# Gate and up products of feed-forward steps 2 to 10 written turned (weights stationary), in a two-block float32 transformer kernel

## The reference

```
def swiglu(x, w_gate_up, w_down):
    g, u = jnp.split(x @ w_gate_up, 2, axis=-1)
    return (jax.nn.silu(g) * u) @ w_down

x = layer_norm(ALPHA * x + mixed, ln1_g[i], ln1_b[i])
x = layer_norm(ALPHA * x + swiglu(x, w_gate_up[i], w_down[i]), ln2_g[i], ln2_b[i])
```

## Time and profile before

| | us |
|---|---|
| median of 3 runs | 1559.26 (1557.5 to 1559.66) |
| span of the profiled execution | 1558.9 |
| TensorE busy | 1537.2 |
| VectorE busy | 1084.7 |
| ScalarE busy | 757.7 |

### The profile page before, as it was taken

How to read it: one execution, slowest core, us unless ns; L and a number is a source line. 1 busy time by engine, 2 the same in 40 slices (tenths; PEclk the granted TensorE clock), 3 DMA queues, 4 the chain that set the end, 5 groups by cost and what they waited for, 6 DMA issues and landing times.

```text
span 1558.9 us, 19900 instructions
## 1 busy us (share of the span) xinstructions
PE 1537.2 (99%) x8187; PEld 1274.7 (82%) x8187; DVE 1084.7 (70%) x1422; ACT 757.7 (49%) x963; POOL 52.7 (3%) x89
## 2 busy tenths in 40 slices
PE   9999999999999999999999999999999999999997
PEld 7887788888878888888788888877888888978986
DVE  6876967656677776675966756888767677567764
ACT  5646544443444434346644343566444434474463
POOL 1100000000000000000000000000100000000010
PEclk9999999999999999999999999999999999999999
DMA  8752567645425766452476664533766546433530
GB/s 317 246 205 79 204 230 256 268 163 189 163 82 197 274 246 255 147 202 96 176 243 243 243 221 152 202 109 136 266 256 233 225 164 223 162 110 147 217 122 27
DMA packets 45898, 299.87 MB, mean 192 GB/s; under 512 B 5540, under 2 KB 5796, under 8 KB 12528
## 3 DMA queue, kind: packets, MB, share of 16 engines
q1 hardware_dynamic: 39600, 278.74, 48.9%
q0 software_dynamic: 5776, 19.01, 3.7%
q10 hardware_dynamic: 432, 0.85, 0.1%
HBM read 296.20 MB, written 2.65 MB: 192 GB/s over the span
## 4 chain that ended last, share of the span: by engine, by line
PE 85%; DVE 8%; ACT 3%; issue 2%; DMA 1%; SPq 0%; POOL 0%; POOLq 0%; DVEq 0%; ACTq 0%
PE psum L1305 53%; PE psum L1264 15%; PE psum L1299 7%; PE psum L1164 3%; DVE w_low L1779 2%; PE psum L1234 1%; PE psum L1428 1%; PE psum L1321 1%; PE psum L1382 1%; PE psum L1416 1%; PE psum L1302 1%; ACT w_high L1533 1%; DMA kv_outside<-arena 1%; DVE xt_low L1813 0%; DVE x_rows L1877 0%
## 5 line engine op out<-in xcount | busy, mean ns | idle before, releaser
L1533 ACT ACTIVATE w_high<-w_raw 128x2048 fp32r<-128x2048 f32 (+1 forms) x240 | 456.5, 1903 | 236.2 <-DMA w_raw<-in_weights 148.9
L1779 DVE TENSOR_TENSOR w_low<-w_raw,w_high 128x2048 fp32r<-128x2048 f32 (+2 forms) x240 | 530.0, 2214 | 34.1 <-ACT w_high L1533 33.3
L1305 PE MATMUL psum<-w_high,xt_high 128*128 128x512 f32 (+1 forms) x1376 | 379.3, 396 | 1.0 <-DVE x_rows L1877 0.8
L1305 PE MATMUL psum<-w_high,xt_low 128*128 128x512 f32 (+1 forms) x1376 | 368.8, 388 | 0.3 <-DVE xt_low L1813 0.3
L1305 PE MATMUL psum<-w_low,xt_high 128*128 128x512 f32 (+1 forms) x1376 | 368.1, 388 | 0.0
L1305 PEld LDWEIGHTS psum<-w_high,xt_low 128*128 128x128 f32 x1376 | 257.9, 188 | 54.9 <-DVE xt_low L1813 0.7
L1305 PEld LDWEIGHTS psum<-w_low,xt_high 128*128 128x128 f32 x1376 | 257.4, 188 | 53.9 <-DVE w_low L1765 0.4
L1305 PEld LDWEIGHTS psum<-w_high,xt_high 128*128 128x128 f32 x1376 | 250.4, 189 | 51.9 <-DVE x_rows L1877 2.4
L2109 DVE TENSOR_TENSOR arena<-arena,psum 128x256 f32<-128x256 f32 x88 | 37.0, 420 | 203.9 <-ACT arena L1665 203.5
L1665 ACT ACTIVATE arena<-psum 128x256 f32<-128x256 f32 x88 | 33.7, 383 | 217.6 <-PE psum L1305 217.6
L1264 PE MATMUL psum<-w_high,ht_high 128*128 128x512 f32 x352 | 99.9, 401 | 0.0
(11 more groups left out here) (250 smaller groups left out, 1486.2 us busy)
## 6 DMA issues: line engine op xcount, KB each, us to landing
w_raw<-in_weights SPq DMA_DIRECT2D x260, 1024.0 KB, 4.8
norm_params<-in_ln_g POOLq DMA_DIRECT2D x8, 512.0 KB, 4.1
norm_params<-in_ln_b POOLq DMA_DIRECT2D x8, 512.0 KB, 5.7
w_raw<-in_weights SPq DMA_DIRECT2D x4, 656.0 KB, 6.0
kv_outside<-arena POOLq DMA_DIRECT2D x3, 512.0 KB, 5.6
mem_kv<-kv_outside POOLq DMA_DIRECT2D x3, 512.0 KB, 3.6
norm_params<-mods_outside POOLq DMA_DIRECT2D x3, 512.0 KB, 6.7
x_rows<-in_x SPq DMA_DIRECT2D x4, 256.0 KB, 5.3
```

Of the source, the lines that this page charges most:

```text
L1305: m = e.matmul(psum[:, bank, 0:w], rows[:, kk, rb * P:rb * P + P], right[:, at:at + w], start=first, stop=last)
L1533: e.activation(K.w_hi[:, g % RING, 0:w], K.w_raw[:, r, 0:w], ACT.Copy).then_inc(K.high.hit(t), 1)
L1779: m = e.tensor_tensor(K.w_lo[:, s, 0:n], K.w_raw[:, r, 0:n], K.w_hi[:, s, 0:n].bitcast(F32), ALU.subtract)
```

## The change

Steps 2 to 10 of each feed-forward part (9 x 4 = 36 steps) take `block_up` in place of `block`. The high and low turned rows become one tensor, `xt_both`. Product n of a half (n is the half of the 256 hidden columns) makes gate and up of 128 hidden columns, turned, in two banks. First come 8 matmuls with `w_hi` stationary (128 x 128) and 512 columns moving, the 256 high and the 256 low turned rows side by side; then 8 with `w_lo` stationary and the 256 high rows moving, added to the first half of the bank. So columns 0 to 255 of a bank hold high x high + low x high, and columns 256 to 511 high x low. Product 0 uses both banks of ring `gemms`, product 1 both banks of ring `tr`.

`gate_turned` replaces `gate`: ScalarE copies columns 256 to 511 of both banks to `ff_rest`; VectorE adds columns 0 to 255 for gate and then for up, and each addition frees its bank; ScalarE takes silu of the gate sum after the first addition; VectorE multiplies. The result is turned already. From step 2 on `split_h` replaces `turn_h`: no transposes, the same high and low halves read from `ff_h`.

`ada_row` moves from right after the block to behind the down products of the step.

```
+    def block_up(self, layer, step, gen):
+        uses = [(ring.take(), ring.take()) for ring in (self.gemms, self.tr)]
+        for half in range(2):
+            t = self.tile("w_gate_up", layer, step, "up", 4 * half)
+            for n in range(2):
+                self.gemm(t, n, half, gen, ("gemm", "turn")[n], uses[n], "up")
+                if half:
+                    self.add("gate_turned", Up(layer, step, n, uses[n], t))
+                self.on()
...
         def turn(step):
-            self.ff_turn[layer, step] = self.tr.take()
-            self.add("turn_h", (layer, step))
+            if step < BY_ROWS:
+                self.ff_turn[layer, step] = self.tr.take()
+                self.add("turn_h", (layer, step))
+            else:
+                self.add("split_h", (layer, step))
...
-        for step in range(2, FF_STEPS):
+        for step in range(BY_ROWS, FF_STEPS):
             if step == 2:
                 self.add("ada_ones", layer)
-            self.block("w_gate_up", layer, step, gen, gate(step), "up")
-            self.ada_row()
+            self.block_up(layer, step, gen)
...
-            if step == 9 and layer in (1, LAST):
-                self.add("modulation", layer // 2)
             turn(step - 1)
             if step < FF_STEPS - 1:
                 if step > 2:
                     t = down_tile(step - 3)
                     for rb in range(RB):
                         down(step - 3, t, rb)
                         self.on()
+                self.ada_row()
+                if step == 9 and layer in (1, LAST):
+                    self.add("modulation", layer // 2)
                 if 2 < step < 9:
                     self.ada_tile()
...
+    def gemm_up(j, hi, lo):
+        ring = (K.gemms, K.tr)[j.rb]
+        if j.half == 0:
+            for use in j.use:
+                pe.wait_ge(*ring.free(use))
+        banks = [psum[:, ring.place(use), :] for use in j.use]
+        for r in range(RB):
+            use = plan.xt_uses[j.gen, r, j.half]
+            pe.wait_ge(*K.xt_high.at(use))
+            pe.wait_ge(*K.tr.out(use))
+        work = [(4 * j.half + k, b, k * BLK + b * FF_STEP + j.rb * P) for k in range(4) for b in range(2)]
+        pe.wait_ge(*K.high.at(j.tile))
+        for kk, b, c in work:
+            e.matmul(banks[b].rearrange("p (n s) -> p n s", n=2), hi[:, c:c + P], K.xt_both[:, :, kk, :], start=kk == 0, stop=False)
+        pe.wait_ge(*K.taken.at(j.tile))
+        for kk, b, c in work:
+            m = e.matmul(banks[b][:, 0:SEQ], lo[:, c:c + P], K.xt_both[:, 0, kk, :], start=False, stop=kk == KC - 1)
+        m.then_inc(K.multiplied.hit((j.tile, j.rb)), 1)
```

ScalarE's part of `gate_turned`, and then VectorE's:

```
+    def gate_turned(j):
+        ring = (K.gemms, K.tr)[j.n]
+        first = min(ring.place(use) for use in j.uses)
+        act.wait_ge(*K.multiplied.at((j.tile, j.n)))
+        if j.step > BY_ROWS:
+            act.wait_ge(*K.h_made.at((j.layer, j.step - 1, j.n)))
+        e.activation(K.ff_rest[j.n], psum[:, first:first + 2, SEQ:BLK], ACT.Copy).then_inc(K.rest_out.hit((j.layer, j.step, j.n)), 1)
+        act.wait_ge(*ring.out(j.uses[0]))
+        e.activation(K.ff_silu[j.step % 2][:, j.n, :], K.ff_gate(j), ACT.Silu).then_inc(K.silu_done.hit((j.layer, j.step, j.n)), 1)
...
+    def gate_turned(j):
+        ring = (K.gemms, K.tr)[j.n]
+        v.wait_ge(*K.rest_out.at((j.layer, j.step, j.n)))
+        for use, row in zip(j.uses, (K.ff_gate(j), K.ff_up(j))):
+            e.tensor_tensor(row, psum[:, ring.place(use), 0:SEQ], row, ALU.add).then_inc(ring.sem(use), 1)
...
+        v.wait_ge(*K.silu_done.at((j.layer, j.step, j.n)))
+        e.tensor_tensor(K.ff_h[j.step % 2][:, j.n, :], K.ff_silu[j.step % 2][:, j.n, :], K.ff_up(j),
+                        ALU.mult).then_inc(K.h_made.hit((j.layer, j.step, j.n)), 1)
```

More of the change, by code:

```diff
@@ L39 @@
 FF_STEPS = D_FF // FF_STEP
+BY_ROWS = 2
 ALPHA = float((2 * len(KINDS)) ** 0.25)
@@ L53 @@
 N_TILES = (3 * KINDS.count("A") + len(KINDS) * (2 * (5 + 1 + 2) + 3 * FF_STEPS) + DEPTH_2 * 2 * (6 + 8 + 2))
-BOTH = ("turned", "memory", "tail", "queries")
+BOTH = ("turned", "memory", "tail", "queries", "up")
 BESIDE = MEMW + IDX_H + HD
@@ L145 @@
 Ff = namedtuple("Ff", "layer step rb use tile")
+Up = namedtuple("Up", "layer step n uses tile")
 Ada = namedtuple("Ada", "row use")
@@ L1246, in gemm @@
         hi, lo = K.w_hi[:, s, :], K.w_lo[:, s, :]
+        if j.kind == "up":
+            gemm_up(j, hi, lo)
+            return
         if j.kind == "down":
@@ L1257, in gemm @@
                 elif n == 1:
-                    pe.wait_ge(*K.tr.out(plan.ff_turn[j.gen[1], j.half]))
+                    pe.wait_ge(*(K.tr.out(plan.ff_turn[j.gen[1], j.half]) if j.half < BY_ROWS
+                                 else K.ht_low.at((j.gen[1], j.half))))
                 else:
@@ L1675, in turn_h, with split_h @@
                      ACT.Copy).then_inc(K.ht_high.hit(j), 1)
+    def gate_turned(j):
[7 more added lines that the diff above has]
+        e.activation(K.ff_silu[j.step % 2][:, j.n, :], K.ff_gate(j), ACT.Silu).then_inc(K.silu_done.hit((j.layer, j.step, j.n)), 1)
+    def split_h(j):
+        layer, step = j
+        if step > 3:
+            act.wait_ge(*K.multiplied.at((plan.down_tile[layer, step - 4], 1)))
+        for n in range(2):
+            act.wait_ge(*K.h_made.at((layer, step, n)))
+        e.activation(K.ht_hi[step % 4], K.ff_h[step % 2], ACT.Copy).then_inc(K.ht_high.hit(j), 1)
     def ada_halves(row):
@@ L1746, in scalar_program @@
               "turn": turn, "dots": dots, "exps": exps, "recip": recip, "turn_prob": turn_prob, "weigh": weigh, "mix_split": mix_split,
-              "gate": gate, "turn_h": turn_h, "ada_halves": ada_halves, "rms": rms, "ret_weigh": ret_weigh, "sb_scores": sb_scores,
+              "gate": gate, "turn_h": turn_h, "gate_turned": gate_turned, "split_h": split_h, "ada_halves": ada_halves, "rms": rms, "ret_weigh": ret_weigh, "sb_scores": sb_scores,
               "sb_halves": sb_halves, "sb_later": sb_later, "sb_split": sb_split, "final": final,
@@ L2116, in turn_h, with split_h @@
                         K.ht_hi[at].bitcast(F32), ALU.subtract).then_inc(K.tr.sem(use), 1)
+    def gate_turned(j):
[3 more added lines that the diff above has]
+            e.tensor_tensor(row, psum[:, ring.place(use), 0:SEQ], row, ALU.add).then_inc(ring.sem(use), 1)
+        if j.step - 2 < BY_ROWS:
+            v.wait_ge(*K.turned.at(plan.ff_turn[j.layer, j.step - 2]))
+        else:
+            v.wait_ge(*K.ht_low.at((j.layer, j.step - 2)))
+        v.wait_ge(*ring.out(j.uses[1]))
+        v.wait_ge(*K.silu_done.at((j.layer, j.step, j.n)))
+        e.tensor_tensor(K.ff_h[j.step % 2][:, j.n, :], K.ff_silu[j.step % 2][:, j.n, :], K.ff_up(j),
+                        ALU.mult).then_inc(K.h_made.hit((j.layer, j.step, j.n)), 1)
+    def split_h(j):
+        at = j[1] % 4
+        v.wait_ge(*K.ht_high.at(j))
+        e.tensor_tensor(K.ht_lo[at], K.ff_h[j[1] % 2], K.ht_hi[at].bitcast(F32),
+                        ALU.subtract).then_inc(K.ht_low.hit(j), 1)
     def ada_ones(layer):
@@ L2287, in vector_program @@
               "choose": choose, "scores": scores, "recip": recip, "turn_prob": turn_prob, "weigh": weigh, "mix_split": mix_split, "gate": gate,
-              "turn_h": turn_h, "ada_ones": ada_ones, "ada_halves": ada_halves, "ada": ada, "modulation": modulation, "norm_rows": norm_rows, "rms": rms,
+              "turn_h": turn_h, "gate_turned": gate_turned, "split_h": split_h, "ada_ones": ada_ones, "ada_halves": ada_halves, "ada": ada, "modulation": modulation, "norm_rows": norm_rows, "rms": rms,
               "modulate": modulate, "rotate": rotate, "ret_scores": ret_scores, "ret_norm": ret_norm,
@@ L2474, in __init__ @@
         self.w_lo = sb("w_low", [P, RING, TW], F32R)
-        self.xt_hi = sb("xt_high", [P, KC, SEQ], F32R)
-        self.xt_lo = sb("xt_low", [P, KC, SEQ], F32R)
+        self.xt_both = sb("xt_both", [P, 2, KC, SEQ], F32R)
+        self.xt_hi, self.xt_lo = self.xt_both[:, 0, :, :], self.xt_both[:, 1, :, :]
         self.x = sb("x_rows", [P, RB, D])
@@ L2520, in __init__ @@
         self.ada_acc = ff[12:14]
+        self.ff_rest = [work[:, BLK * n:BLK * n + BLK].rearrange("p (b s) -> p b s", b=2) for n in range(2)]
         self.prob = [work[:, 1024 * n:1024 * n + 1024] for n in range(2)]
@@ L2609, in __init__ @@
         self.divided, self.mixed_high, self.mixed_low = signal("divided"), signal("mixed_high"), signal("mixed_low")
-        self.silu_done, self.ht_high = signal("silu_done"), signal("ht_high")
+        self.silu_done, self.ht_high, self.ht_low = signal("silu_done"), signal("ht_high"), signal("ht_low")
+        self.rest_out, self.h_made = signal("rest_out"), signal("h_made")
         self.ld_scale, self.ld_norm_g, self.ld_shift = signal("ld_scale"), signal("ld_norm_g"), signal("ld_shift")
@@ L2715, in group_on_scalar, with ff_gate, ff_up @@
         return 0 if by_rows(j) and self.unit_pieces(j) > 4 else None
+    def ff_gate(self, j):
```

(5 more changed lines are left out.)

## The result

The changed kernel takes 1604.23 us (1604.08 to 1606.92), the kernel before 1559.39 us. The ratio is 1.0297, 95% interval 1.0284 to 1.0310: slower by 45 us, where 26 were forecast.

What follows compares the result with a forecast made beforehand. TensorE, busy 99% of the span, was taken to bound the kernel. Span 1558.9 - 8.3 (TensorE's work) + 20.4 (ada row) + 13.6 (start of a part) = 1584.6, with 0.4 to the median 1585.0 us; range 1568 to 1606.

Steps and rivals of the forecast that it cites:

- rival C: TensorE's granted clock falls behind each of 12 new idle times, 1.7 us each: 1605 us; chance 16%.
- TensorE's own work: Blocks of 36 steps cost 7.6 us more, the transposes removed save 15.8 us: net 8.3 us less.
- The chain behind a product: VectorE's queue after a block runs 1.6 us later in every step, free in steps without an ada row.
- rival D: VectorE's queue has no room left and some 27 steps slip by 0.5 to 1 us: 1600 to 1612; chance 6%.
- The ada row: Next block's second product waits for VectorE's late ada addition in steps 5 and 7 of four parts: 20.4 us.
- The start of a part: At steps 1 to 3, TensorE idles 0.46, 2.43 and 0.5 us for banks: 3.4 us per part, 13.6 in all.
- The wait for `ht_low`: At the start of each part, a product wants the bank of step 1's transposes: 0.5 us idle.
- The clock: TensorE's granted clock after new idle times: a fall costs 1.7 us, but the sum included none.
- Rival A: The bank waits don't bite and only TensorE's matmul and transpose savings count: 1551 us; chance 7%.

Runs made afterwards that it cites:

- e7: The kernel before with the four transposes of steps 2 to 10 made twice into the same bank: 1573.94 us against 1557.88.
- e3: The changed kernel with the ada row between the two down products and the transposes of step 1 ahead of the block of step 2: 1556.68 us.
- e4: The changed kernel with 8 more matmuls (a repeated high-weight pass) just ahead of each wait for the ada row, 64 in all: 1596.29 us.
- e2: The changed kernel with the transposes of step 1 ahead of the block of step 2, not behind it: 1590.36 us.
- e1: The changed kernel with the ada row between the two down products of its step, not behind both: 1569.93 us.
- e5: The changed kernel with the ada row back right behind the block, turned products kept: 1592.02 us.

## Why the prediction was right or wrong

Sign, mechanism and places were right; the central number lay 19 us low, and the range held the result at its upper end (1604 of 1606), for the most part for the reason that rival C gave. That it held it was in part luck: 4 of the 12 long waits brought no fall of the clock, and had they brought one too, at some 1.45 us each, the time would have been some 1610 us, outside the range.

- **TensorE's own work**: forecast -8.3 us. The block measured 11.14 instead of 11.09 (36 x 0.26 = 9.4 us more), the transposes -15.8, confirmed by e7 as -16.1: -6.4 to -6.7. e3 with its small waits left comes out 1.9 us under the kernel before. The 13 ns per matmul that the rows of before showed held: the Trainium skill's 2.5 ns (TensorE: Matmul & The Clock Gate, "Back-to-back issue gap") doesn't agree with this trace. By it the whole would have come out some 6 us lower, and the row was the better guide. The Trainium skill gives that figure for a single isolated matmul, which the prediction left out, and these matmuls stand in a stream.
- **The chain behind a product**: `low` at T + 2.39, measured T + 2.40. A step without an ada row lost nothing, so rival D (no room on VectorE) didn't happen; VectorE still idled 1.76 us between two gates.
- **The ada row**: 8 waits of 2.55 us forecast, 2.75 measured, 22.0 us in all against 20.4. Step 9 lost nothing, as forecast.
- **The start of a part**: 2.43 us forecast, 2.58 measured (10.3 us), and 0.5 us at the gate of step 1. The wait for `ht_low` was put at 0.5 us in four parts and was 0.4 in two: in the other two parts the clock had fallen, and TensorE came to the bank too late to wait for it.
- **The clock**: this is the step that failed. The sum took no fall of the clock, and rival C, with 12 falls and 16%, was judged by "full blocks stand on both sides". 8 of 12 waits brought one. One costs some 1.45 us (3.51 against 2.06 for the same eight matmuls), less than the 1.7 of the forecast, since part of the low clock falls into the idle time (the clock was 0.60 over 275 to 276 us, and TensorE began only at 275.50); e4 saved 7.9 us at the six of the ada rows.

Together: -6.4 for TensorE's own work and 35.1 for the four groups of waits make 28.7 us, and the span grew by 43.4. The 14.7 us between are for the most part the clock's: 8 falls x 1.45 us are 11.6, one of them lasted twice as long (some 1.4 more), and 1.7 us are left. They are of the size of what the list of waits doesn't count: from the start of the eight 256-column matmuls at 271.64 to the next start at 275.50 it is 3.86 us, where a steady step has 0.95, so 2.91 us are lost for 2.75 listed. At the start of a part it is 2.75 for 2.58. Over the 12 long waits that makes some 2 us.

The forecast went from the span to the time by adding 0.4 us, the distance in the kernel before. In the changed kernel the median lies 1.9 us over the profiled span (1604.23 and 1602.3), and the profiled execution's own time 1.8 (1604.08). So the span of 1558.9 us most likely belonged to an execution slower than the median; no time of it is on record. Of the 19.2 us missed, 1.9 are TensorE's own work, 1.1 the listed waits, 14.7 the clock with the rest above, and 1.5 this step from span to time.

Rival A (faster) needed VectorE at the ada addition by T + 8.7; it was there at T + 10.6. e3 shows how near one comes to A once the order is changed: 1556.7 us, where A had 1551.

## What to carry to other kernels

When a change makes a stage ask for a buffer earlier or for more of them, walk the queue of the engine that gives the buffer back and read off when its release comes up; an engine that is idle 30% of the time can still be late, because its order is fixed. The cure is then an order, not a faster engine: moving one step of the list brought back 34 us. Add the clock to the price of TensorE's idle times: between full blocks those of 2.6 and 2.75 us brought falls here, those of 1.9 us or less none (nothing between was tried). And let e3 be the measure of the idea itself: of the transposes' 16 us, over half (9.4) go into the 16 additional matmuls per block.

## What the runs showed of the hardware that was not expected

An idle time of TensorE of 2.75 us between full blocks was followed by a granted clock at the 1.2 GHz level in 6 of 8 places of the changed kernel and in 5 of 8 of e2. At the start of a part, 2.6 us, it was 2 of 4 in the changed kernel, 1 of 4 in e1, 2 of 4 in e4 and 2 of 4 in e5. Behind 1.55 us it was none of 12 (e5), and behind 0.93 (six times), 1.56 and 1.90 us (once each) none of 8 (e4). The same wait at the same step differs from place to place and from run to run, so its length doesn't decide alone; what else does, no run here shows. In one place of the changed kernel (the second ada row of the fourth part) and one of e2 (the second of the first part) the low clock lasted past the first eight matmuls.

Where TensorE does little between them, shorter idle times were followed by a fall too. The one of the earlier trace rows, behind short sets of transposes and idle times of 1.07 and 0.73 us, stands at the same place in the traces of the kernel before, the changed kernel, e4 and e5, and is missing in the other six. So a single trace of this kernel can hold it or not, and at some 1.5 us it is worth nearly as much as the whole gain of e3.

The Trainium skill (TensorE: Matmul & The Clock Gate, "What's actually happening") has activity releasing the throttle; the runs agree, in that no fall followed in e4, where 1.8 us of matmuls were added ahead of each idle time (0 of 8, against 6 of 8).
